# Taking the 32 sample rows out of the seven output products and giving them fp32 products on quarters of the array's columns

## The reference, cut to what matters

```
h = rms_norm(x) * norm_pre
p = h @ w_in                      # three head groups, each with a gate
mixed = concat(o_A*silu(g_A), o_B*silu(g_B), o_C*silu(g_C))   # (rows, 2048)
y = x + rms_norm(mixed @ w_out) * norm_post                   # w_out (2048, 2048)
```

## Time and profile before

| what | value |
|---|---|
| median of 3 runs | 1926.81 us (1926.7 to 1927.8) |
| the profiled execution's own time | 1926.09 us |
| its span in the trace | 1924.3 us |
| granted TensorE clock, mean | 0.998 |
| TensorE matmul busy | 1892.5 us, 98% |
| VectorE busy | 1255.5 us, 65% |
| ScalarE busy | 676.8 us, 35% |

### The profile page before, as it was taken

How to read it: one execution, slowest core, us unless ns; L and a number is a source line. 1 busy time by engine, 2 the same in 40 slices (tenths; PEclk the granted TensorE clock), 3 DMA queues, 4 the chain that set the end, 5 groups by cost and what they waited for, 6 DMA issues and landing times.

```text
span 1924.3 us, 31225 instructions
## 1 busy us (share of the span) xinstructions
PE 1892.5 (98%) x12592; PEld 1752.7 (91%) x12592; DVE 1255.5 (65%) x2251; ACT 676.8 (35%) x1245; POOL 53.7 (3%) x119
## 2 busy tenths in 40 slices
PE   6999999999999999999999999999999999999997
PEld 5999999999999999999999999999999988888886
DVE  7368787787878778554454455465426666866878
ACT  7234334343433434122222222233213354344453
POOL 4000000000000000000000000000000000000131
PEclk9999999999999999999999999999999999999999
DMA  6456777676777767666657667465446657555396
GB/s 246 118 120 138 160 158 167 145 148 155 149 164 154 163 147 155 148 138 144 145 124 157 136 143 143 110 140 128 105 97 143 140 204 279 194 173 186 121 263 223
DMA packets 885063, 301.57 MB, mean 157 GB/s; under 512 B 623160, under 2 KB 850248, under 8 KB 883624
## 3 DMA queue, kind: packets, MB, share of 16 engines
q1 hardware_dynamic: 881848, 290.86, 62.1%
q0 software_dynamic: 3072, 8.73, 2.2%
HBM read 210.45 MB, written 96.20 MB: 159 GB/s over the span
## 4 chain that ended last, share of the span: by engine, by line
PE 88%; DVE 8%; ACT 1%; issue 1%; DMA 1%; POOL 0%; DVEq 0%; SPq 0%; ACTq 0%; POOLq 0%
PE ps L1272 22%; PE ps L1273 20%; PE ps L1274 20%; PE ps L1473 4%; PE ps L1475 4%; PE ps L1474 4%; PE ps L1364 3%; PE ps L1444 3%; PE ps L1414 2%; PE ps L1336 2%; DVE arena L1965 1%; DVE act_lo L1832 1%; DVE arena L1825 1%; PE ps L1470 1%; PE ps L1469 1%
## 5 line engine op out<-in xcount | busy, mean ns | idle before, releaser
L1272 PE MATMUL ps<-act_hi,w_hi 128*128 128x352 f32 x2688 | 878.1, 327 | 0.2
L1274 PE MATMUL ps<-act_hi,w_lo 128*128 128x352 f32 x2688 | 863.4, 321 | 0.0
L1273 PE MATMUL ps<-act_lo,w_hi 128*128 128x352 f32 x2688 | 863.2, 321 | 0.0
L1272 PEld LDWEIGHTS ps<-act_hi,w_hi 128*128 128x128 f32 x2688 | 504.8, 188 | 20.1 <-issue 15.5
L1273 PEld LDWEIGHTS ps<-act_lo,w_hi 128*128 128x128 f32 x2688 | 505.7, 188 | 0.0
L1274 PEld LDWEIGHTS ps<-act_hi,w_lo 128*128 128x128 f32 x2688 | 504.7, 188 | 0.0
L1574 ACT ACTIVATE w_hi<-w_raw 128x512 fp32r<-128x512 f32 x224 | 139.4, 624 | 374.3 <-DMA w_raw<-in_w_in_dram 374.2
L1840 DVE TENSOR_TENSOR w_lo<-w_raw,w_hi 128x512 fp32r<-128x512 f32 x224 | 150.6, 673 | 53.1 <-ACT w_hi L1574 52.9
L1641 ACT ACTIVATE arena<-arena,small 128x257 f32<-128x257 f32 (+6 forms) x180 | 101.3, 566 | 198.6 <-DVE small L2003 198.6
L2191 DVE STREAM_TRANSPOSE arena<-arena 128x1024 f32<-128x1024 f32 (+4 forms) x100 | 132.6, 1326 | 37.7 <-ACT arena L1781 36.9
L1781 ACT ACTIVATE arena<-arena 128x1024 f32<-128x1024 f32 (+1 forms) x60 | 61.1, 1019 | 236.5 <-DVE arena L1977 236.4
(11 more groups left out here) (190 smaller groups left out, 2114.3 us busy)
## 6 DMA issues: line engine op xcount, KB each, us to landing
w_raw<-in_w_in_dram SPq DMA_DIRECT2D x176, 256.0 KB, 3.4
weight_scratch<-arena SPq DMA_DIRECT2D x216, 128.0 KB, 3.4
arena<-weight_scratch SPq DMA_DIRECT2D x54, 512.0 KB, 4.6
b_out<-in_w_out_dram SPq DMA_DIRECT2D x72, 256.0 KB, 3.3
w_raw<-in_w_out_dram SPq DMA_DIRECT2D x70, 256.0 KB, 2.7
w_raw<-in_w_in_dram SPq DMA_DIRECT2D x96, 128.0 KB, 3.0
weight_scratch<-arena SPq DMA_DIRECT2D x80, 132.0 KB, 4.0
arena<-weight_scratch SPq DMA_DIRECT2D x40, 256.0 KB, 3.3
```

What stands on the lines that cost most here:

```text
L1272: mm(bank(g, GN), wh, ah, start=(k == 0), stop=False)
L1273: mm(bank(g, GN), wh, al, start=False, stop=False)
L1274: last = mm(bank(g, GN), wl, ah, start=False, stop=(k == KT - 1))
```

## The change

The fifth group goes: products 3, 2, 4 and 5 keep four groups, and `ls`, `ls_f` and their splitting, copying and adding go with it. Instead, sixteen times, after pieces 10, 15, ... 85 (`SAMPLE_AFTER`), TensorE takes the sample rows' raw fp32 block k as a 32-column stationary and multiplies it with whole rows of w_out in fp32: four products of 512 columns, each on its own quarter of the array's columns and of PSUM's partitions (`sample_out`). SP loads those 128 rows of w_out whole, 128x2048, into one buffer `w_s`, as soon as the previous block has been used (`rows_out`). All sixteen accumulate in bank 7, so the other groups rotate through seven banks. At the end ACT copies the four quarters into `y_s` (`sample_copy`).

```diff
 def evac_at(s, j):
...
-    return at_piece(KH * s + KH - 1 + (j + 1) / GROUPS_IN[s] + 0.1)
+    return at_piece(KH * s + KH - 1 + (j + 1) / 4 + 0.1)
...
+def sample_at(v):
+    return at_piece(SAMPLE_AFTER[v] + 1)
...
+def squares_at(t, n):
     if t == TT:
-        return stage_of((4, 5)[n // 2], n % 2)
...
+        return sample_at(KT - 1) + 2.0 + 0.5 * n
...
-    for n in range(3):
-        at = TICKS - 0.4 if n == 0 else at_piece(12 + 2 * n)
-        if engine == "dve" and n == 1:
-            plan.append((at - 1.0, "sample_sum", 0, n))
-        elif engine == "act":
-            plan.append((at, "sample_hi", 0, n))
-        if engine == "dve":
-            plan.append((at + 0.8, "sample_lo", 0, n))
+    for n in range(KT):
+        if engine == "sp":
+            plan.append((sample_at(n - 1) if n else at_piece(6), "rows_out", 0, n))
+    for n in range(NCH):
+        if engine == "act":
+            plan.append((sample_at(KT - 1) + 0.1 * n, "sample_copy", 0, n))
...
-SAMPLE_OF = {3: 0, 2: 1, 4: 2, 5: 1}
+SAMPLE_ORDER = tuple(range(KH, KT)) + tuple(range(KH))
+SAMPLE_AFTER = [10 + 5 * v for v in range(KT)]
+SAMPLE_BANK = 7
...
+            def rows_out(v):
+
+                if v:
+                    sp.wait_ge(s_used, v)
+                else:
+                    sp.wait_ge(proj_done, 3 * TILES)
+                sp.dma_start(w_s[:, :], w_out_v[:, K_ROWS[SAMPLE_ORDER[v]], :]).then_inc(s_in, 16)
...
-                if k == 0 and g >= 8:
-
-                    before = GROUP[g - 8]
+                if k == 0 and g >= SAMPLE_BANK:
+
+                    before = GROUP[g - SAMPLE_BANK]
...
-                if j == 4:
-                    if first:
-                        pe.wait_ge(ls_low, SAMPLE_OF[m] + 1)
-                    both = ls[SAMPLE_OF[m]][:, 2 * DEC * k:2 * DEC * k + P]
-                    mm(out, both, wh, start=first, stop=False)
-                    last = mm(out, both, wl, start=False, stop=end)
...
+            def sample_out(v):
+
+                k = SAMPLE_ORDER[v]
+                pe.wait_ge(s_in, 16 * (v + 1))
+                pe.wait_ge(mixed_in[LOAD_OF[k]], 16)
+                for j in range(NCH):
+                    last = mm(ps[DEC * j:DEC * j + DEC, 512 * SAMPLE_BANK:512 * SAMPLE_BANK + PIECE], raw[:, k, SEQ:TOK],
+                              w_s[:, PIECE * j:PIECE * j + PIECE], start=(v == 0), stop=(v == KT - 1), skip_group_check=True)
+                last.then_inc(s_used, 1)
...
             for r in range(LEAD):
-                for j in (3, 4):
-                    out_mm(r, j)
+                out_mm(r, 3)
             for r in range(LEAD, TAIL0):
                 operands_out(r)
-                for j in range(GROUPS_IN[r // KH]):
+                for j in range(4):
                     out_mm(r, j)
+                if r in SAMPLE_AFTER:
+                    sample_out(SAMPLE_AFTER.index(r))
...
+            def sample_copy(n):
+                act.wait_ge(s_used, KT)
+                fn(y_s[0:DEC, PIECE * n:PIECE * n + PIECE], ps[DEC * n:DEC * n + DEC, 512 * SAMPLE_BANK:512 * SAMPLE_BANK + PIECE],
+                   ACT.Copy).then_inc(s_copied, 1)
```

More of the change, by code:

```diff
@@ L540 @@
 STAGE = [(ORDER[s // 2], s % 2) for s in range(STAGES)]
[L541 to L545, removed]
+G0 = [4 * s for s in range(STAGES + 1)]
+GROUP = [(s, j) for s in range(STAGES) for j in range(4)]
+COPIED = {(s, j): int(STAGE[s][0] in TILE_COPIES) for s, j in GROUP}
+ADDS = {(s, j): len(TILE_ADDS[STAGE[s][0]]) for s, j in GROUP}
 COPIES_BY = dict(zip(GROUP, itertools.accumulate(COPIED[g] for g in GROUP)))
@@ L652, in build @@
         l_sum = [place(f"l_sum{k}", [P, 512], F32, 0, c + 512) for k, c in enumerate(LEFT_AT)]
-        ls = [place(f"ls{i}", [P, 576], F32R, 0, 11008 + 576 * i) for i in range(3)]
-        ls_f = [place(f"ls_f{i}", [P, 576], F32, 0, 11008 + 576 * i) for i in range(3)]
         y_s = place("y_s", [P, D], F32, 0, 12736)
+        w_s = place("w_s", [P, D], F32, 0, 12736)
         r_extra = [place(f"r_extra{i}", [P, PIECE], F32, 0, 14784 + PIECE * i) for i in (0, 1)]
@@ L1235, in _ @@
                     mixed_load(n)
+                elif what == "rows_out":
+                    rows_out(n)
                 elif what == "post_gains":
@@ L1462, in out_mm @@
                     pe.wait_ge(proj_out, 3 * (TILES - 1) + g + 1)
-                out, wh, wl = bank(g % 8), r_hi(r), r_lo(r)
+                out, wh, wl = bank(g % SAMPLE_BANK), r_hi(r), r_lo(r)
                 first, end = k == 0, k == KH - 1
-                if j == 4:
-                    if first:
-                        pe.wait_ge(ls_low, SAMPLE_OF[m] + 1)
-                    both = ls[SAMPLE_OF[m]][:, 2 * DEC * k:2 * DEC * k + P]
-                    mm(out, both, wh, start=first, stop=False)
-                    last = mm(out, both, wl, start=False, stop=end)
-                else:
-                    th, tl = l_hi[k][:, P * j:P * j + P], l_lo[k][:, P * j:P * j + P]
-                    mm(out, th, wh, start=first, stop=False)
-                    mm(out, th, wl, start=False, stop=False)
-                    last = mm(out, tl, wh, start=False, stop=end)
+                th, tl = l_hi[k][:, P * j:P * j + P], l_lo[k][:, P * j:P * j + P]
+                mm(out, th, wh, start=first, stop=False)
+                mm(out, th, wl, start=False, stop=False)
+                last = mm(out, tl, wh, start=False, stop=end)
                 if end:
                     last.then_inc(y_done, 1)
-                elif j == GROUPS_IN[s] - 1:
+                elif j == 3:
                     last.then_inc(r_used, 1)
+            def sample_out(v):
[6 more added lines that the diff above has]
+                last.then_inc(s_used, 1)
             def operands_out(r):
@@ L1756, in _ @@
                     left_high(u, n)
-                elif what == "sample_hi":
-                    sample_high(n)
+                elif what == "sample_copy":
+                    sample_copy(n)
                 elif what == "copy":
@@ L2168, in _ @@
                     left_low(u, n)
-                elif what == "sample_lo":
-                    sample_low(n)
                 elif what == "add":
```

98 lines of the change are left out of this document (24 added, 74 removed).

## The result

The kernel after takes 1929.76 us in the median of 22 runs (1926.44 to 1934.61), the kernel before 1927.14 us in the median of 22 runs beside it. The ratio is 1.0016, 95% interval 1.0009 to 1.0022: slower, by less than the 0.2% that was taken for the limit of what can be told. The forecast was 1921.2 us. The profiled execution of the kernel after is its slowest run, 1934.61 us with a span of 1932.9.

A forecast was written before the change was run, and what follows sets the result against it. TensorE was taken to bound the output phase, with thin places at its start and in stages 11 and 12. -29.1 + 19.2 + 2.3 + 2.0 = -5.6 us gave 1920.5 profiled, 1921.2 as median; range 1917 to 1932.

The forecast's parts named there:

- What goes and what comes: In TensorE's queue, 128 matmuls go, 29.1 us; sixteen visits of four fp32 products come, 1.20 us each, 19.2 us.
- Rival A: In the visits, never more than two records in flight: 2.04 us each, sixteen 32.6, total 1934.6; chance 0.15.
- the five-step case: In a visit, second records hold up the next quarter's first: 2.47 us each, total 1941.5; with one-by-one, chance 0.07.
- Piece 6: At the output phase's start, TensorE wants this piece 2.7 us earlier, its DMA traffic stays: a wait of 2.3 us.
- Edits costed at nothing: Sixteen 1 MB loads, seven banks instead of eight, and earlier sample copies, squares and finish add no time of their own.
- six-deep ring: Pieces in stages 2 to 5 are loaded 13.6 us ahead of use, leaving their users some 8 us in hand.
- rival B: Each megabyte load makes TensorE wait 0.6 us through late pieces or adds: 9.6 us, total 1930.8; chance 0.08.
- Late stretch: In stages 11 and 12, DVE's 70 instructions need 42.8 to 47.9 us: 2.0 us given back, 4.7 at worst.
- Tail: After TensorE's last matmul, the ending is the prompt's and stays; the sample's earlier finish counts for nothing.
- Same: The measured time can't be told from no change, neither below 1923.0 nor above 1930.7 us; chance 0.22.
- Rival C: All 4.7 us given back in the late stretch and 2 more around piece 10: 1925.9, no change; chance 0.17.

The follow-up runs named there:

- again: The kernel after, unchanged, timed and profiled once more: 1928.55 us, ratio 1.0012 to the kernel before.
- fill_early: The kernel after with the three copies of the input into the output issued in the projection phase: 1923.62 us, ratio 0.9986 to the kernel before.
- before_fill: The kernel before with the three copies of the input into the output issued in the projection phase: 1926.97 us, ratio 1.0002.
- rows_once: The kernel after with `w_s` loaded once instead of sixteen times, all visits kept: 1925.21 us, ratio 0.9990 to the kernel before.
- small_gains: `fill_early` with eight prompt gains (and four behind piece 104) made on 2 columns instead of 512: 1924.69 us, ratio 0.9988 to the kernel before.
- finish_late: `fill_early` with the sample's squares, gains and end at piece 102.5: 1924.22 us, ratio 0.9989 to the kernel before.

## Why the prediction was wrong

The forecast was a gain of 5.6 us and the kernel lost 2.6 in the medians, 3.2 in the profiles. Two steps failed: the periodic loads costed at nothing, and the size of the loss in stages 11 and 12. The sum of the forecast beside the profile of `again` (1929.33 us, 3.2 above the profiled 1926.09 of before):

| term | forecast | shown |
|---|---|---|
| 128 matmuls removed | -29.1 | -29.1 |
| sixteen visits | +19.2 | +19.6 |
| start: piece 6 | +2.3 | +4.6 |
| piece 56 | 0 | +3.1 |
| stages 11 and 12, beyond the 1.4 before | +2.0 | +6.0 |
| behind the last matmul | 0 | -1.6 |
| output phase begins later | | +0.6 |
| sum | -5.6 | +3.2 |

Shown are, in order: a stage with a fifth group is 25.39 in before and 21.76 without one, so 3.63 x 8; 24.21 less 21.76 for two visits, so 1.225 x 16; stage 0 from piece 3, 18.15 less 13.60; stage 7, 26.19 less the 23.13 that it takes in `fill_early`; 50.96 less 43.52 and less 1.44; 9.1 less 10.7. The last, 0.6, lies ahead of all that was changed in this phase: the first matmul of piece 0 starts at 1578.01 in the profile of before, at 1578.49 in that of `before_fill`, at 1578.64 in that of `again` and between 1577.94 and 1578.90 in all, so it is scatter. Of the 8.8 us between forecast and profile, the late stretch has 4.0, piece 56 has 3.1 and the start 2.3; the tail gives 1.6 back.

- **What goes and what comes: right.** The step from two halves to four quarters had no row, and it held to 2%: 1.225 us against 1.20. Rival A falls. An estimate by the 3.07 that the Trainium skill (TensorE: Matmul & The Clock Gate, Measured speedup vs the span model) gives for four row tiles made the sixteen visits 23.0 us; they are 19.6, so the measurement decides for the greater overlap. The same page of the Trainium skill (What overlaps and what doesn't) has matmuls start and end in strict program order. Here the first records of the four products start 7 ns apart in order, the second ones 0.43 us later, so none waits for a second record of the product before it; the five-step case that the prediction derived from it doesn't occur.
- **Piece 6: mechanism and place right, size short.** In the 13 profiles of this kernel and its variants with this wait it is 2.3 to 4.0 us long, mostly 2.4 to 2.8, against 2.3. Not foreseen was the clock: seven to thirteen matmuls at 1.2 GHz behind seven of the 13, 1.4 to 2.7 us. The sum had no term for it.
- **"Edits costed at nothing": failed.** With the next step this turned the sign. The cover named was some 8 us in hand by the six-deep ring and a DMA share of 0.57 in stages 2 to 5. The 8 us and the 0.57 were read in a quiet stage and carried to all sixteen loads. In stage 6 three copies of the input, which before met DMAs with room left (0.73 and 0.86), meet the megabyte loads (0.99); a piece takes 12 us, ACT waits 7.09, and the copies that free banks stand behind it. The text named this very chain ("DVE waits in order for a late piece and the bank-freeing adds wait behind it") and didn't look for the transfer that would start it. It is rival B at one place instead of sixteen: 3.1 us, not 9.6. Either party alone costs nothing (`before_fill`, `fill_early`, `rows_once`).
- **Late stretch: mis-sized, and its worst case too low.** Forecast 2.0 out of 4.7 at most (no wait of DVE's closing up), shown 4.9 to 6.0; in `again` 1.4 of the 6.0 is the lower clock behind the wait before piece 94. The bound was DVE's 70 instructions, 42.8 us, with its waits thought to close up by about half. They didn't: the adding transfers hold the DMAs, pieces land in 6.7 us, and DVE with less work waits for them (2.08 us in `small_gains`). The prediction had read the DMA share of 1.07 and gave it no term of its own; with the adding transfers narrowed 2.9 us of the loss went.
- **Tail: failed, to the good.** 1.6 us gained by the sample's end moving forward (`finish_late` loses it again).
- **Chances.** "Same" had 0.22 and is what came. That 1929.76 lies within the range of 1917 to 1932 is luck: the range reached that far for rivals that lose time in other places or amounts, and the tail's gain of 1.6 us, which wasn't forecast, hides a part of the misses. Rival C had the right direction for the late stretch and the wrong place for the rest (around piece 10 nothing waits).

What stays open: why some waits are followed by slow matmuls and others aren't (1.95 and 2.82 in `again` are, 2.93 in the same profile isn't; 3.39 in `fill_early` isn't either). Whether eight banks would have kept the collision off TensorE wasn't run. The time of the adding transfers wasn't shortened with their work kept, so whether the 5 us are to be had in a whole kernel wasn't tried.

## What to carry to other kernels

Before costing a new periodic transfer at nothing, walk through the issue list of the whole stretch where it repeats and look for the one-off transfers that it will meet: the average DMA share of a quiet stage speaks for that stage alone. In engines that work strictly in order, follow a late piece to the bank-freeing work behind it. Where a bottleneck engine's queue gets shorter, ask of each thin place which resources are full there, and take each away by itself and all together: moving one wait (a bank, eight gains) only showed the next. Before reading a difference of 1 or 2 us between two profiles, compare the granted clock of the two stretches: a stretch at the lower clock behind a wait cost 1.4 to 2.9 us here, in some executions of the same kernel and not in others.

## What the hardware showed that was not expected

- Four fp32 products of 512 columns on four quarters of the array's columns take as long as one: 0.87 us for eight records (0.99 less 0.12 for the way out), against 0.89 for the two records of one.
- After a wait TensorE can run at 1.2 GHz for seven to fourteen matmuls of 0.43 us. It followed waits of 3.63, 3.70 and 6.19 us, and some as short as 1.95 (`again`, piece 94) and 2.31 (`small_gains`, piece 6), but not those of 2.93, 2.92 and 3.39. In the output phase before the change no wait was over 0.65 us, and none was followed by it.
- Adding transfers into DRAM issued by GpSimd took 11.0 and 13.2 us for 512 KB at the median, with the DMAs nearly full, and 61.7% of the DMA engines for 2.55 MB, where 2.72 MB of the other transfers took 34.8%.
